# Four groups of prompt tiles instead of three, and one pace for the experts over all of them

## The reference

```python
h = LN(x) * (1 + scale1) + shift1                 # shift, scale, gate from c @ w_ada
gq, gk, gv, glr, gog, sq, sk, sv, mg_a, mg_b = split_cols(h @ w_in)
branch_a = gla(gq, gk, gv, glr, gog) @ w_gla_proj # 4 heads, gated linear attention, carries a state
branch_b = stick_breaking(sq, sk, sv) @ w_sb_proj # 16 heads x 64, causal; the samples also see 1024 cached keys
mix = (sigmoid(mg_a) * branch_a + sigmoid(mg_b) * branch_b) @ w_o
x  = LN1(alpha * x + gate1 * mix)
h2 = LN(x) * (1 + scale2) + shift2
# PEER: per token and head (8 heads) the best 16 of 128 x 128 experts by two half keys
w  = softmax(top16) * gelu(peer_u[ids] . h2)      # rows of peer_u are gathered
x  = LN2(alpha * x + gate2 * sum(w * peer_v[ids]))# rows of peer_v are gathered
```

## Time and profile before

| | us |
|---|---|
| median of three runs | 4868.33 (4856.72 to 4876.36) |
| the profiled execution | 4863.06 |
| its span in the trace | 4861.2 |
| TensorE matmul busy | 3451.5 (71%) |
| VectorE busy | 2755.5 (57%) |
| GpSimd busy | 2549.8 (52%) |
| ScalarE busy | 930.4 (19%) |
| DMA | 1580.58 MB, mean 325 GB/s |

### The profile page before, as it was taken

How to read it: one execution, slowest core, us unless ns; L and a number is a source line. 1 busy time by engine, 2 the same in 40 slices (tenths; PEclk the granted TensorE clock), 3 DMA queues, 4 the chain that set the end, 5 groups by cost and what they waited for, 6 DMA issues and landing times.

```text
span 4861.2 us, 46453 instructions
## 1 busy us (share of the span) xinstructions
PE 3451.5 (71%) x16090; PEld 1711.0 (35%) x16090; DVE 2755.5 (57%) x6532; ACT 930.4 (19%) x2008; POOL 2549.8 (52%) x2359
## 2 busy tenths in 40 slices
PE   5787989887888879877899887799763333333355
PEld 3354665454544534333444345444320000000000
DVE  2233331358986765567777766644787666664420
ACT  2244230013442210011444422200110000000000
POOL 0000000005466666656677665656577777777775
PEclk8798999988999989988999998899875555555565
DMA  5766223339899999999999998989999999999997
GB/s 226 292 233 232 95 85 124 117 143 333 283 333 333 362 374 393 416 351 400 347 405 394 326 357 329 362 346 417 354 357 389 404 394 383 397 392 400 419 401 307
DMA packets 445319, 1580.58 MB, mean 325 GB/s; under 512 B 48328, under 2 KB 87624, under 8 KB 434720
## 3 DMA queue, kind: packets, MB, share of 16 engines
q0 software_dynamic: 338080, 1231.18, 65.9%
q1 hardware_dynamic: 105104, 344.78, 19.2%
q10 hardware_dynamic: 1904, 1.65, 0.1%
HBM read 1527.99 MB, written 49.43 MB: 324 GB/s over the span
## 4 chain that ended last, share of the span: by engine, by line
PE 41%; POOL 17%; DMA 16%; DVE 12%; issue 9%; ACT 4%; ACTq 0%; SPq 0%; DVEq 0%; POOLq 0%
DMA peer_v_ring<-in_peer_v,expertsT 11%; POOL peer_v_ring L2326 9%; POOL peer_u_ring L2318 8%; PE bank L2386 6%; PE wide L1356 5%; PE wide L1775 4%; PE wide L2057 4%; PE bank L713 3%; DVE peer_u_ring L2477 3%; PE wide L1344 3%; PE bank L1775 2%; PE wide L778 2%; PE bank L723 1%; PE wide L788 1%; DMA mod_w<-in_w_ada 1%
## 5 line engine op out<-in xcount | busy, mean ns | idle before, releaser
L2318 POOL DMA_INDIRECT peer_u_ring<-in_peer_u,experts x1152 | 1287.3, 1117 | 820.9 <-DVE peer_u_ring L2477 409.1
L2477 DVE SCALAR_TENSOR_TENSOR peer_u_ring<-peer_u_ring,peer_h 128x1024 f32<-128x1024 f32 x1152 | 1385.4, 1221 | 526.3 <-DMA peer_u_ring<-in_peer_u,experts 482.9
L2386 PE MATMUL bank<-peer_v_ring,peer_lone 128*32 128x512 f32 x4608 | 853.9, 823 | 941.0 <-DMA peer_v_ring<-in_peer_v,expertsT 825.1
L2326 POOL DMA_INDIRECT peer_v_ring<-in_peer_v,expertsT x1152 | 1232.9, 1070 | 477.5 <-issue 296.7
L2386 PEld LDWEIGHTS bank<-peer_v_ring,peer_lone 128*32 128x32 f32 x4608 | 115.4, 124 | 1527.1 <-issue 1479.7
L2287 POOL MEMSET peer_lone<- 128x1087 f32 x1 | 1.0, 1003 | 984.3 <-SPq L269 984.3
L1356 PE MATMUL wide<-w_ring,hT 128*128 128x256 f32 x1152 | 278.3, 401 | 32.8 <-DVE gla_v L1694 32.8
L713 PE MATMUL bank<-hT,w_ring 128*128 128x384 f32 x768 | 264.9, 494 | 18.2 <-DMA w_ring<-in_weights 15.9
L2057 PE MATMUL wide<-mT,w_ring 128*128 128x384 f32 x768 | 269.6, 501 | 10.4 <-DMA w_ring<-in_weights 7.4
L1356 PEld LDWEIGHTS wide<-w_ring,hT 128*128 128x128 f32 x1152 | 228.6, 202 | 100.9 <-issue 67.8
L1121 DVE SCALAR_TENSOR_TENSOR sb_l<-sb_z,sb_l 128x768 f32<-128x768 f32 (+2 forms) x120 | 95.5, 796 | 169.4 <-ACT sb_l L996 169.1
(11 more groups left out here) (281 smaller groups left out, 4544.5 us busy)
## 6 DMA issues: line engine op xcount, KB each, us to landing
w_ring<-in_weights SPq DMA_DIRECT2D x312, 512.0 KB, 6.6
sb_kc<-in_kcT SPq DMA_DIRECT2D x16, 2048.0 KB, 11.6
sb_vc<-in_vc SPq DMA_DIRECT2D x16, 2048.0 KB, 7.3
mod_w<-in_w_ada SPq DMA_DIRECT2D x24, 1024.0 KB, 5.9
peer_u_ring<-in_peer_u,experts POOLq DMA_INDIRECT x1152, 6.5
peer_v_ring<-in_peer_v,expertsT POOLq DMA_INDIRECT x1152, 6.4
scores<-sel_sc SPq DMA_DIRECT2D x6, 1024.0 KB, 8.9
peer_sc_half<-scores POOLq DMA_DIRECT2D x12, 512.0 KB, 7.6
```

Source lines behind the costliest of these rows:

```text
L2318: pool.indirect_dma_start(self.u_ring[:, n % NU, :], None, K.A["peer_u"], bass.IndirectOffsetOnAxis(ap=K.ids_of[:, j % CHOSEN, k:k + 1], a ...
L2326: pool.indirect_dma_start(self.v_ring[:, m % NV, :], None, K.A["peer_v"], bass.IndirectOffsetOnAxis(ap=K.ids_of_turned[:, j % CHOSEN, t:t ...
L2386: last = pe.matmul(self.F.psum[strip:strip + 32, :], self.lone[:, mark - at:mark - at + 32], self.v_ring[:, m % NV, c * HALF:(c + 1) * HAL ...
L2477: dve.scalar_tensor_tensor(u, u, 1.0, self.h2[:, j % 2, :], ALU.mult, ALU.mult, accum_out=self.dots[:, j % 2, k:k + 1]).then_inc(self.dot_ ...
```

## The change

The groups are cut anew. Before: tiles 0, 1 and the samples; tiles 2 to 4; tiles 5 to 7. After: tile 0 and the samples; tiles 1 and 2; tiles 3 and 4; tiles 5 to 7. The first group has then one prompt step in each pair, so the hand-written orders leave out the second (`second = G.hi > 1`) and count steps by `G.hi * p`. `paces()` no longer spreads each group's slots over that group alone: it draws one line through all groups, as steep as the limits at the groups' ends allow, and weights are kept as they were. Worked out, the list has these slots at the ends of the stages:

| group | stick | gla | mix | res | select |
|---|---|---|---|---|---|
| before: second, tiles 2-4 | 150 | 232 | 306 | 330 | 370 |
| before: third, tiles 5-7 | 551 | 627 | 695 | 717 | 754 |
| after: second, tiles 1-2 | 83 | 127 | 179 | 192 | 220 |
| after: third, tiles 3-4 | 325 | 368 | 420 | 433 | 461 |
| after: fourth, tiles 5-7 | 600 | 657 | 709 | 725 | 753 |

Before, a slot comes every 2.2 units of weight in the second group and every 2.45 in the third; after, every 3.2 units in all. The weights of mix and select don't depend on the width of a group. The buffer wait of `key_scales` in gla is written for groups with any number of prompt tiles.

```diff
-GROUPS = grouped(((0, 2, True), (2, 5, False), (5, 8, False)))
+GROUPS = grouped(((0, 1, True), (1, 3, False), (3, 5, False), (5, 8, False)))
...
-    out = [0] * marks[0]
-    for n, here in enumerate(marks[:-1]):
-        stop = marks[n + 1]
-        before, to = max(0, SLOTS * GROUPS[n].first - MARGIN), SLOTS * GROUPS[n + 1].first - MARGIN
-        total, done = sum(units[here:stop]), 0.0
-        for w in units[here:stop]:
-            done += w
-            out.append(int(before + (to - before) * done / total))
+    out, n, slots, at = [0] * marks[0], 0, 0.0, sum(units[:marks[0]])
+    ends = [(m, sum(units[:m]), SLOTS * g.first - MARGIN) for m, g in zip(marks, GROUPS)]
+    while n + 1 < len(ends):
+        slope, n = min(((to - slots) / (when - at), m) for m, (_, when, to) in enumerate(ends) if m > n)
+        for w in units[len(out):ends[n][0]]:
+            at += w
+            slots += slope * w
+            out.append(int(slots))
+    for m, g in zip(marks[1:], GROUPS[1:]):
+        assert out[m - 4 * PEER_HEADS - 4] > SLOTS * (g.first - 2) + Select.NAME_AT
...
-            i, u = 2 * p, 2 * p
+            i, u, second = G.hi * p, 2 * p, G.hi > 1
...
-            self.scores(pe, G, i + 1)
+            if second:
+                self.scores(pe, G, i + 1)
```

The last six lines stand for the same edit at each call with `i + 1`, on TensorE, ScalarE and VectorE. In `key_scales`:

```diff
-        if h or n >= 2:
-            at = self.tile(G, h, n - 2) if n >= 2 else self.tile(G, h - 1, G.np + n - 2)
+        before = h * G.np + n - 2
+        if before >= 0:
+            at = self.tile(G, before // G.np, before % G.np)
             act.wait_ge(self.att_bank(at).full, self.att_bank(at).full_at["att", at])
```

More of the change, by code:

```diff
@@ L910, in tensor_early @@
             next(ahead, None)
-            self.to_here(pe, G, i + 1)
+            if second:
+                self.to_here(pe, G, i + 1)
             self.c_values(pe, G, u)
             next(ahead, None)
-            self.later_keys(pe, G, i + 1)
+            if second:
+                self.later_keys(pe, G, i + 1)
             next(ahead, None)
-            self.values(pe, G, i + 1)
+            if second:
+                self.values(pe, G, i + 1)
             self.c_out_turn(pe, G, u)
@@ L1092, in scalar_early @@
             self.weights(act, G, i)
-            self.take_z(act, G, i + 1)
+            if second:
+                self.take_z(act, G, i + 1)
             if more:
@@ L1096, in scalar_early @@
             self.c_weights(act, u)
-            self.log_z(act, G, i + 1)
+            if second:
+                self.log_z(act, G, i + 1)
             self.c_take(act, G, u + 1)
             self.c_take_log(act, u + 1)
-            self.weights(act, G, i + 1)
+            if second:
+                self.weights(act, G, i + 1)
             if more:
@@ L1190, in vector_early @@
             self.exponent(dve, G, i)
-            self.softplus(dve, G, i + 1)
+            if second:
+                self.softplus(dve, G, i + 1)
             self.c_keep_turned(dve, u)
             self.c_sums(dve, u + 1)
-            self.exponent(dve, G, i + 1)
+            if second:
+                self.exponent(dve, G, i + 1)
             self.c_keep_values(dve, u)
@@ L1497, in key_scales @@
             here = n * P
-            before = self.b[:, here + s * SUB - 1:here + s * SUB] if s else 0.0
-            last = act.activation(self.kl[:, m % 2, s, 0:(s + 1) * SUB], self.b[:, here:here + (s + 1) * SUB], ACT.Exp, bias=before, scale=-1.0)
+            start = self.b[:, here + s * SUB - 1:here + s * SUB] if s else 0.0
+            last = act.activation(self.kl[:, m % 2, s, 0:(s + 1) * SUB], self.b[:, here:here + (s + 1) * SUB], ACT.Exp, bias=start, scale=-1.0)
         last.then_inc(self.kl_exp, 1)
```

## The result

The changed kernel takes 5004.64 us (5000.58 to 5021.7), the kernel before 4862.83 beside it: a ratio of 1.0294, 95% interval 1.026 to 1.0329. On two other chips the ratio was 1.0221 (1.0194 to 1.0247) and 1.0259 (1.0239 to 1.0279). The forecast was 5040, in a range of 4850 to 5130 that begins at no change.

The account below looks back on a forecast made before the run. TensorE bounds the head, DMA the tail, both nearly the middle (TensorE's chains in stick and gla, bytes in mix). Head -199, middle +371, tail unchanged: +172 on 4863.1 gives 5035, 5040 as median; range 4850 to 5130.

Parts of the forecast that it names:

- The head: First group's stages before the expert slots start: one tile fewer, bounded by TensorE's work, saves 199 us, bounds 150 and 240.
- Gla: First group's gla: a third of 188 us front work is 63, the sample's serial part stays, so 50 us saved.
- The middle: Groups after the first, beside the expert slots: three groups instead of two take 2856 us for 2484.5, +371.
- gla of the third group: Tiles 3 and 4: 125 us front work, 24 for 42 values, 47 idle, together 196 us.
- The step that failed in its reason: Mix of the two narrow groups: bytes at 397 GB/s set 172 and 184 us; the tail is a DMA stretch.
- the faster rival: Transfers decide: the middle takes 2650 us at 360 GB/s, total 4834; holds if the middle is under 2683; chance 0.12.
- The step that failed in its size: TensorE's work moved into the middle: one tile's 242 us, 2317 us busy in all, with no extra for narrower groups.
- A narrower group costs TensorE nothing in itself: Projections: time scales with columns, so a third of the columns takes a third of the time.
- The one that kept TensorE's share at 0.835: Rival for the middle: 2317 us of TensorE work at the old share gives 2775 us, total 4959; chance 0.15.
- The clock did not fall to 0.85 in the narrow sticks: Rival: narrow groups' stick and gla at clock 0.85 rather than 0.92 take 57 us more, total about 5160; chance 0.06.
- The Trainium skill's case of matmul bursts shorter than the DMA waits between them: Narrow groups' mix: the clock would fall back to half, but 138 us of TensorE work would still fit into 172.
- The pace: Even slot spreading, counted within the numbers: 3.1 us a slot in the new second group against 4.2 in the last.

Follow-up runs that it names:

- the run with two banks: The changed kernel with both heads' score tiles in two PSUM banks in all groups without samples: 5079.52 us against 5112.23, ratio 1.0202; 1.0185 on another chip.
- The two mended costs: The changed kernel with score tiles in two PSUM banks and mix and stick weights by group width, together: 5053.8 us against 5102.37, ratio 1.0143.
- the slots by width: The changed kernel with weights of mix and of stick's half steps that go with the group's width: ratio 1.0173 to the kernel before.

## Why the prediction was right, and where it was not

**The head.** Forecast -199 us, measured -230.7. Stick gave 39.3 (50 forecast), mix 56.0 (57), res 17.3 (22), select 23.7 (20). Gla was mis-sized: 243.2 to 151.7 us, 91.5 instead of 50. A tile costs TensorE 71 us there (212.0 less 140.7), not 63, and 20 us of idle went with it. In the old first group TensorE waited 17.2 us in its by-token matmuls for VectorE to empty a bank; three tiles need two bank fills for v and for og, two tiles one. In the new one no such wait is left. This was read and argued, not tested. The wait, in the kernel before from 497.0 to 740.2 us:

```profile
PE wide L1356 <- DVE gla_v L1694: 17.2, 3, 5.7
```

The first dot came at 873.6 us, for 902 expected and 1101.4 before.

**The middle.** Forecast 2856 us, measured 2850.7. By groups, norm included: 741.6 for 730, 879.2 for 912, 1229.9 for 1214. By stages the nearest were stick (200.5 for 198, 329.1 for 335, 511.5 for 522); gla of the third group was 164.3 for 196. The forecast there had kept 47 us idle of the wide group, and 14.5 remained.

**The step that failed in its reason.** The forecast read the tail as a DMA stretch and put mix of the narrow groups at 172 and 184 us, by bytes at 397 GB/s. Measured were 184.0 and 175.0, the other way round, but weights' bytes and row bytes were each shown to be worth 2 to 11 us of it, and TensorE was busy 151.8 and 143.5 us there, for under 145. In the tail it is gathers that count: GpSimd needs 1.01 us for an instruction (937.63 by 927) and up to 0.30 to the next, and two of them make 2.6 of the 2.7 us that two take there (1264.8 by 463.5). In mix that is the likely reading, not a shown one. The sum stood because bytes and gathers go together, 1.05 MB for two gathers. By the same error the faster rival was priced by bytes. The figure of about 435 GB/s that the Trainium skill gives for the SBUF ports (DMA: Bandwidth & Descriptors, Where 436 GB/s comes from) is not reached over a stage in any run here; the fullest stage shown here moved 402 GB/s, and the fullest in any run's stick, gla, mix, res or select 418, a mix of the new cut with the old pace.

**The step that failed in its size.** "A narrower group costs TensorE nothing in itself" is wrong by 100 us of busy time. The work that went to the middle was 326.6 us, for 242 forecast. 40 us are the score steps, shown by the run with two banks, worth 33 us of time. The forecast's middle was 2317 us of work and 539 of idle, a share of 0.81; measured were 2401 and 449, a share of 0.842. So its work was 84 us too small and its idle 90 us too large. That the middle came out within 5 us is luck, and the head, 32 us better than forecast, makes up most of the 35 us by which the time lies under 5040.

**The rivals.** The faster one needed the middle under 2683 us; it fell, with 82 MB fewer giving 14 us. The one that kept TensorE's share at 0.835 had the share right (0.842) but the work too small: with 2401 us of work it gives 2876 us, nearer than its own 2775. In this respect it described the middle better than the forecast did, at a chance of 0.15 against 0.60. The clock did not fall to 0.85 in the narrow sticks (0.91 and 0.95); in the three glas it was 0.87, 0.95 and 0.86, for 0.91 and 0.90 before. The Trainium skill's case of matmul bursts shorter than the DMA waits between them (TensorE: Matmul & The Clock Gate, HAM oscillation) did not come about in mix: TensorE was busy 151.8 of 184.0 us there, with 12 waits for value rows of at most 2.8 us, at 0.93 of the clock. The prediction said of it that 138 us of work would still fit into 172; at 0.50 of the clock instead of 0.95 they would be 262, an estimate, and would not. The low clocks are in res (0.78 and 0.77), where TensorE waits for VectorE, 21.1 us of the 68.7 in the new second group.

**The pace.** It was called part of the numbers and no cause; the old cut with it is at 0.999, and on the new cut it saves about 0.6%, by the estimate above. The remark that its weights ignore a group's width was worth more than thought: mending it gives about 0.7%, by the same estimate.

Open: the 60 us of busy time outside the score matmuls were not taken apart. The two mended costs are 48.6 of the 117 us that the changed kernel is slower on that chip, by the medians; why the rest is lost is argued from TensorE's share and not shown. Neither the old pace nor the slots by width ran beside the changed kernel on one chip.

## What to carry to other kernels

Cutting work into more groups to start the overlapped part sooner pays only if the engine that takes over the moved work has room where it goes: here TensorE was busy 84% of the middle before and after, so 231 us won at the start were paid for with 366. When an overlapped stream looks bound by bytes, look at the waits of the queue that issues it before pricing it by bytes. A weight list made for one width, and a layout chosen by a width threshold, both need another look when the width changes: the two were worth 1% here.

## What was not expected of the hardware

A tail at a DMA share of 0.99 and 386 GB/s had its pace from GpSimd, which in 800 us of it never waited over 0.7 us. On another chip, where the tail has a share of 0.95, half of each value row left out gave 258 GB/s at a share of 0.79 and 1362.5 us instead of 1340.1. There a gather of half rows took GpSimd as long as one of whole rows, 1.04 and 1.03 us (539.3 and 533.0 us by 519), while the unchanged gathers beside them went from 1.05 to 1.24 us. And the same kernel before took 4862.83 us on one chip and 4983.72 to 5013.03 on others; the changed kernel's tail took 1264.8 and 1340.1 us, its middle 2850.7 and 2883.2, so differences of this kernel are read as ratios on one chip.
